# MoE kernel: the last tile's rows turned first, puts ahead of weight sums, a bank wait moved into the loop, final sums on VectorE alone

## The reference, cut to what matters

```python
    yx = jnp.concatenate([o_hg_x, o_pool_x], axis=-1) @ w_out[l]
    x = x + gt1 * rms_norm(yx, g_post_mix[l])
    hx2 = (rms_norm(x, g_pre_ffn[l]) * (1.0 + sc2) + sh2).reshape(B * S, D)
    # moe(hx2): logits = xt @ w_router + b_router; top 4 of 32, softmax over the four
    # for each token and chosen expert e, with weight w:
    gate = xblk @ w_gate[e] + b_gate[e]
    up = xblk @ w_up[e] + b_up[e]
    gate = jnp.minimum(gate, SWIGLU_LIMIT)
    up = jnp.clip(up, -SWIGLU_LIMIT, SWIGLU_LIMIT)
    h = (up + 1.0) * gate * jax.nn.sigmoid(SWIGLU_ALPHA * gate)
    y = h @ w_down[e] + b_down[e]          # times w, summed over the token's four experts
    x = x + gt2 * rms_norm(y, g_post_ffn[l])
```

## Time and profile before

| | |
|---|---|
| median of 3 runs | 2398.84 us (2397.83 to 2398.97) |
| profiled execution | 2394.5 us, its span 2392.6 us |
| PE busy | 2221.9 us, 93% of the span |
| VectorE, ScalarE, GpSimd busy | 44%, 28%, 16% |
| matmuls of `gate_up` (L1753) | 9216, 1007.7 us busy |
| matmuls of `down` (L1786) | 9216, 508.7 us busy |
| chain that ended last, share of PE | 85% |

### The profile page before, as it was taken

The page is one execution under the profiler, slowest core; times in us unless marked ns, Lnnn a source line. Parts: engine busy times, 40 slices in busy tenths (PEclk is TensorE's granted clock), DMA queues, the critical chain, the costliest instruction groups (busy, mean ns, idle before and its releaser), DMA issues.

```text
span 2392.6 us, 57077 instructions
## 1 busy us (share of the span) xinstructions
PE 2221.9 (93%) x21767; PEld 1176.8 (49%) x21768; DVE 1043.4 (44%) x1664; ACT 668.5 (28%) x1414; POOL 376.6 (16%) x491
## 2 busy tenths in 40 slices
PE   5999999998996599999999999999998999999982
PEld 3485765867454244545445454444443444444441
DVE  4154547445346344434434443443353444433334
ACT  5111222233344332222322222322232222222222
POOL 5000000000014212111111121111122112211111
PEclk9999999999997699999999999999999999999996
DMA  9112011126205294967979788888887897888864
GB/s 302 35 36 72 26 33 48 31 67 246 93 36 202 90 373 127 360 211 279 338 250 344 251 313 314 287 305 287 286 328 272 303 340 271 309 291 337 322 216 157
DMA packets 187702, 525.54 MB, mean 220 GB/s; under 512 B 20330, under 2 KB 68066, under 8 KB 187490
## 3 DMA queue, kind: packets, MB, share of 16 engines
q1 hardware_dynamic: 133874, 338.86, 37.7%
q10 hardware_dynamic: 36240, 134.29, 14.4%
q0 software_dynamic: 17536, 51.69, 9.6%
HBM read 486.21 MB, written 38.57 MB: 219 GB/s over the span
## 4 chain that ended last, share of the span: by engine, by line
PE 85%; DMA 6%; DVE 4%; issue 1%; ACT 1%; POOL 1%; ACTq 0%; SPq 0%; POOLq 0%; DVEq 0%
PE ps L1753 40%; PE ps L1786 19%; PE ps L1536 6%; PE ps L1637 5%; PE ps L1532 5%; DMA w_gu_e<-in_w_up_dram 4%; PE ps L1542 2%; PE ps L1593 2%; PE ps L1539 2%; PE ps L1615 1%; PE ps L1656 1%; PE ps L1508 1%; DMA w_down_e<-in_w_down_dram 1%; DVE box L1107 0%; DVE y_all L1460 0%
## 5 line engine op out<-in xcount | busy, mean ns | idle before, releaser
L1753 PE MATMUL ps<-w_gu_e,xT 128*32 128x512 f32 x9216 | 1007.7, 595 | 34.3 <-DVEq L1418 16.6
L1753 PEld LDWEIGHTS ps<-w_gu_e,xT 128*32 128x32 f32 x9216 | 355.9, 110 | 667.4 <-issue 667.1
L1786 PE MATMUL ps<-w_down_e,hT 128*32 128x256 f32 x9216 | 508.7, 380 | 13.4 <-ACT yrow L932 8.4
L1786 PEld LDWEIGHTS ps<-w_down_e,hT 128*32 128x32 f32 x9216 | 351.3, 110 | 181.8 <-issue 40.8
L1383 DVE STREAM_TRANSPOSE gu_t<-ps 128x1024 f32<-128x1024 f32 x94 | 111.9, 1229 | 639.4 <-PE ps L1753 639.4
L914 ACT ACTIVATE xT<-xr,fm 128x128 f32<-128x128 f32 x392 | 184.1, 490 | 569.0 <-PE ps L1753 544.6
L1369 DVE TENSOR_SCALAR yrow<-ps,slot_tab 32x256 f32<-32x256 f32 x376 | 181.3, 482 | 259.0 <-PE ps L1786 167.9
L932 ACT ACTIVATE yrow<-ps,slot_tab 32x256 f32<-32x256 f32 x384 | 179.4, 467 | 352.2 <-issue 235.9
L655 POOL DMA_INDIRECT xg<-xn_rows,idx_g x196 | 197.4, 1007 | 85.4 <-issue 47.6
L649 POOL TENSOR_TENSOR idx_g<-slot_tab,base_row 128x4 int32<-128x4 int32 x49 | 9.2, 189 | 1101.6 <-DVE xr L1405 1087.5
L1536 PE MATMUL ps<-hxT,w_ring 128*128 128x512 f32 (+1 forms) x384 | 142.5, 529 | 3.7 <-ACT hxT L802 3.7
(11 more groups left out here) (301 smaller groups left out, 1515.2 us busy)
## 6 DMA issues: line engine op xcount, KB each, us to landing
w_gu_e<-in_w_gate_dram SPq DMA_DIRECT2D x256, 512.0 KB, 10.7
w_gu_e<-in_w_up_dram SPq DMA_DIRECT2D x256, 512.0 KB, 11.6
w_down_e<-in_w_down_dram ACTq DMA_DIRECT2D x124, 1024.0 KB, 9.2
w_ring<-in_w_ada_dram SPq DMA_DIRECT2D x17, 1024.0 KB, 5.2
w_ring<-in_w_in_dram SPq DMA_DIRECT2D x20, 512.0 KB, 5.2
w_first<-in_w_ada_dram SPq DMA_DIRECT2D x7, 1024.0 KB, 12.2
x_all<-in_x_dram SPq DMA_DIRECT2D x2, 2048.0 KB, 10.6
w_out<-in_w_out_dram SPq DMA_DIRECT2D x8, 512.0 KB, 8.6
```

What stands on the lines that cost most here:

```text
L1753: last = T.matmul(ps[j * GROUP:(j + 1) * GROUP, g, :].rearrange("p (w b f) -> p w b f", w=2, f=GROUP), xT[:, k, g * GROUP:(g + 1) * GROUP] ...
L1786: last = T.matmul(ps[j * GROUP:(j + 1) * GROUP, 4 + g // 2, g % 2 * QUARTER:(g % 2 + 1) * QUARTER], hT[:, g, k, :], w_dn[:, k, j * QUARTER ...
```

## The change

It does five things.

1. For the last tile, PE turns the rows of tile 7 first, then does places(5) and logits(6). VectorE does place(5) ahead of choose(6), and ScalarE exponents(5) ahead of the copy of tile 7, without calling the square root in between.
2. GpSimd puts the slots of tiles 5, 6 and 7 in a row, and sums their weights behind them.
3. PE no longer waits for all 16 copies of the first rows ahead of the loop. ScalarE raises `gu_evac` by 2 when it has issued the last of them, and the waits on `gu_evac` in `gate_up` and on VectorE are 2 higher.
4. `down` asks for size > 0 first, around the rest, and `apart` stands behind all branches, where it stood only in that of size 0 and 1.
5. The final sums are all VectorE's: y * gain for each tile as it lands, into a buffer of its own, `yg_all`; then, by group, yg * rstd + x in one instruction. The groups are of 2, 3 and 3 tiles instead of 1, 2, 2 and 3.

```diff
@@ -157,7 +157,7 @@
         r = region(0, 64)
         w_gu = r("w_gu_e", 2, KT, D)
         w_dn = region(72, 104)("w_down_e", KT, D)
-        y_all = region(0, 32)("y_all", TL, D)
+        y_all, yg_all = region(0, 32)("y_all", TL, D), region(32, 64)("yg_all", TL, D)
 
         r = region(141, 149)
         xg, xr = r("xg", GROUPS, QUARTER), r("xr", GROUPS, KT, GROUP)
@@ -352,8 +352,7 @@
         Y0_BANK = (4, 5, 2, 3)
         TAB_AT, ORD_AT = 0, 4 * NTAB
 
-        FIN = ((0, 1), (1, 3), (3, 5), (5, 8))
-        FIN_POOL = (2, 4, 6)
+        FIN = ((0, 2), (2, 5), (5, 8))
 
 
         vec_in, x_in, misc_in = sem("vec_in"), [sem(f"x_in{k}") for k in range(3)], sem("misc_in")
@@ -395,8 +394,8 @@
             sem(n) for n in ("w_full_ready", "wT_psum", "wT_ready", "y0_psum", "y0_ready"))
         b_dn_in, y0_out = sem("b_dn_in"), [sem(f"y0_out{b}") for b in range(len(y0_sb))]
         y_added = sem("y_added")
-        fin_sq, fin_scaled, fin_dve, fin_pool, out_done = (
-            sem(n) for n in ("fin_sq", "fin_scaled", "fin_dve", "fin_pool", "out_done"))
+        fin_sq, fin_gained, fin_dve, out_done = (
+            sem(n) for n in ("fin_sq", "fin_gained", "fin_dve", "out_done"))
 
 
         Y_ZERO = 1
@@ -531,10 +530,7 @@
             for t in range(TL):
                 sp.dma_start(y_all[:, t, :], y_dram[t * P:(t + 1) * P, :]).then_inc(y_in[t], 16)
             for t in range(TL):
-                if t in FIN_POOL:
-                    sp.wait_ge(fin_pool, FIN_POOL.index(t) + 1)
-                else:
-                    sp.wait_ge(fin_dve, sum(u not in FIN_POOL for u in range(t + 1)))
+                sp.wait_ge(fin_dve, t + 1)
                 sp.dma_start(out[0, t * P:(t + 1) * P, :], x1[:, t, :]).then_inc(out_done, 16)
             sp.wait_ge(out_done, 16 * TL)
 
@@ -631,8 +627,12 @@
                 G.tensor_tensor(w_full[:, t, :], w_j[:, 0, :], w_j[:, 1, :], ALU.add).then_inc(w_full_ready, 1)
                 pool.wait_ge(w_full_ready, t + 1)
 
-            for t in range(TL):
+            for t in range(TL - 3):
                 put_slots(t)
+                spread_weights(t)
+            for t in range(TL - 3, TL):
+                put_slots(t)
+            for t in range(TL - 3, TL):
                 spread_weights(t)
             for k in range(2):
                 pool.wait_ge(xn2_out[k], 16 * TL // 2)
@@ -683,9 +683,6 @@
             scatter(n_before)
             scatter(n_last)
             pool.wait_ge(xg_in, n_last * (16 * GROUPS) + 3 * 16 * GROUPS)
-            for t in FIN_POOL:
-                pool.wait_ge(fin_scaled, t + 1)
-                G.tensor_tensor(x1[:, t, :], x1[:, t, :], y_all[:, t, :], ALU.add).then_inc(fin_pool, 1)
 
 
         @block.scalar
@@ -872,9 +869,11 @@
                 root(ROOT_YX + 1 + 2 * t, 0, 1)
                 if t >= 3:
                     exponents(t - 3)
+                if 3 <= t < TL - 1:
                     A.activation(rs_s[:, 39:40], ones[:, 0:1], ACT.Sqrt)
+            exponents(TL - 3)
             transposed_tile(TL - 1)
-            for t in range(TL - 3, TL):
+            for t in range(TL - 2, TL):
                 exponents(t)
 
             def weights_turned(t0, nt):
@@ -903,6 +902,7 @@
             first_rows(0)
             weights_turned(4, 4)
             first_rows(4)
+            act.sem_inc(gu_evac, 2)
 
             def rows_scaled(m):
 
@@ -1268,8 +1268,8 @@
                     choose(t - 2)
                 if t >= 3:
                     place(t - 3)
+            place(TL - 3)
             choose(TL - 2)
-            place(TL - 3)
             choose(TL - 1)
             place(TL - 2)
             place(TL - 1)
@@ -1382,7 +1382,7 @@
                 for half in range(2):
                     V.transpose(guT[:, 2 * half:2 * half + 2].rearrange("p g w b i -> p (g w b i)"),
                                 ps[:, 2 * half:2 * half + 2, :].rearrange("p a n -> p (a n)")).then_inc(gu_evac, 1)
-                dve.wait_ge(gu_evac, m * 2 + 2)
+                dve.wait_ge(gu_evac, m * 2 + 4)
                 both = guT[:].rearrange("p g w b i -> p g (w b) i")
                 g, u = (guT[:, :, w].rearrange("p g b i -> p g (b i)") for w in range(2))
                 lk(V.tensor_tensor(both, both, biasT[:, :, bass.ds(e, 1)].unsqueeze(1).to_broadcast(
@@ -1445,10 +1445,19 @@
                 ins.then_inc(dve_chain, 1)
                 dve.wait_ge(dve_chain, done + (base + n_tail[0]))
 
+            def gained(lo, hi):
+
+                for t in range(lo, min(hi, TL)):
+                    dve.wait_ge(y_in[t], 16)
+                    V.tensor_tensor(yg_all[:, t, :], y_all[:, t, :], gain[1][:], ALU.mult).then_inc(fin_gained, 1)
+
+            gained(0, FIN[0][1])
             for g, (lo, hi) in enumerate(FIN):
+                gained(lo + 1 if g else hi, hi)
                 dve.wait_ge(fin_sq, hi)
                 c_ = slice(lo, hi)
                 V.tensor_scalar(rs_v[:, c_], ssq[:, c_], 1.0 / D, EPS, ALU.mult, ALU.add).then_inc(var_ready, 1)
+                gained(hi, hi + 1)
                 dve.wait_ge(root_ready, ROOT_YX + 2 * TL + g + 1)
                 lk(V.reciprocal(rs_s[:, c_], rs_s[:, c_]))
                 lk(V.tensor_tensor(rs_t[:, c_], rs_s[:, c_], rs_s[:, c_], ALU.mult))
@@ -1456,12 +1465,9 @@
                 lk(V.tensor_scalar(rs_t[:, c_], rs_t[:, c_], -0.5, 1.5, ALU.mult, ALU.add))
                 lk(V.tensor_tensor(rstd[:, c_], rs_s[:, c_], rs_t[:, c_], ALU.mult))
                 for t in range(lo, hi):
-                    y = y_all[:, t, :]
-                    V.scalar_tensor_tensor(out=y, in0=y, scalar=rstd[:, t:t + 1], in1=gain[1][:], op0=ALU.mult,
-                                           op1=ALU.mult).then_inc(fin_scaled, 1)
-                    if t not in FIN_POOL:
-                        dve.wait_ge(fin_scaled, t + 1)
-                        V.tensor_tensor(x1[:, t, :], x1[:, t, :], y, ALU.add).then_inc(fin_dve, 1)
+                    dve.wait_ge(fin_gained, t + 1)
+                    V.scalar_tensor_tensor(out=x1[:, t, :], in0=yg_all[:, t, :], scalar=rstd[:, t:t + 1],
+                                           in1=x1[:, t, :], op0=ALU.mult, op1=ALU.add).then_inc(fin_dve, 1)
 
 
         @block.tensor
@@ -1704,14 +1710,14 @@
                     if t >= 2:
                         pe.wait_ge(yx_used, t - 1)
                     yx(t, K_EARLY + K_LATE).then_inc(yx_psum, 1)
-                if 1 <= t < TL:
+                if 1 <= t <= TL:
                     turned_rows(t - 1)
+                if t == TL:
+                    places(t - 3)
                 if 2 <= t < TL + 2:
                     logits(t - 2)
-                if t >= 3:
+                if t >= 3 and t != TL:
                     places(t - 3)
-                if t == TL:
-                    turned_rows(t - 1)
             pe.wait_ge(cum_ready, TL)
             T.matmul(ps[:, 0, TL * NE:(TL + 1) * NE], ones_bf[:], cum_bf[:, TL - 1, :], start=True, stop=True
                      ).then_inc(pos_psum, 1)
@@ -1727,7 +1733,7 @@
 
             def gate_up(m, loaded, size):
 
-                pe.wait_ge(gu_evac, m * 2)
+                pe.wait_ge(gu_evac, m * 2 + 2)
                 apart(pe)
                 with pe.If(size > 1):
                     with pe.If(size > 2):
@@ -1764,17 +1770,17 @@
                 pe.wait_ge(yr_ready, n)
                 pe.wait_ge(yv_ready, n)
                 apart(pe)
-                with pe.If(size > 1):
-                    with pe.If(size > 2):
-                        with pe.If(size == 4):
-                            down_of(loaded, (2, 3), False)
-                        with pe.Else():
-                            down_of(loaded, (2,), False)
-                    down_of(loaded, (0, 1), True)
-                with pe.Else():
-                    with pe.If(size > 0):
+                with pe.If(size > 0):
+                    with pe.If(size > 1):
+                        with pe.If(size > 2):
+                            with pe.If(size == 4):
+                                down_of(loaded, (2, 3), False)
+                            with pe.Else():
+                                down_of(loaded, (2,), False)
+                        down_of(loaded, (0, 1), True)
+                    with pe.Else():
                         down_of(loaded, (0,), True)
-                    apart(pe)
+                apart(pe)
 
             def down_of(loaded, groups, ends):
 
@@ -1792,7 +1798,6 @@
 
             pe.wait_ge(tables, 1)
             n_rounds = rounds(pe)
-            pe.wait_ge(y0_ready, 2 * TL)
             with pe.Fori(0, n_rounds) as n:
                 pair = item_pair(pe, n)
                 down(n, (pair >> 12) * 16, (pair >> 3) & 7)
```

## The result

| | before | after |
|---|---|---|
| median | 2397.93 us (2395.40 to 2398.97, 8 runs) | 2404.57 us (2402.02 to 2407.37, 8 runs) |
| profiled execution, span | 2392.6 us | 2401.5 us |
| last `down` matmul ends | 2345.9 | 2360.3 |
| first loop matmul starts | 807.2 | 804.1 |

The changed kernel takes 1.0029 times as long as the one before (95% interval 1.0018 to 1.0039): it is 6.6 us slower, where 6.6 us less was forecast. All ratios in this document leave out two executions in a slower state, one of 6080 us in e6 and one of 2475.7 us of the kernel before, measured with e9 to e12.

A forecast was written before the change was run, and what follows sets the result against it. The prediction took PE's two matmul lines in the expert loop as the bound, so only edges and joints could move: -7.8 (start) + 6.5 (joints) - 5.3 (final sums) = -6.6, from 2398.8 to 2392.2 us, range 2384 to 2398.

The forecast's parts named there:

- Router, 2.3: Router's last tile: turning tile 7's rows first lets its logits start 2.3 us earlier.
- Bank wait out of line, 3.3: Ahead of the loop: PE loads and branches without waiting for the bank copies, 3.3 us earlier.
- Slot table, 2.2, not in the sum: GpSimd's puts ahead of the sums: slot table 2.2 us earlier, bounds 0.9 and 3.7, not setting the loop's start.
- One branch instead of two, 2.2: Ahead of the loop: empty item 0 of `down` branches once, not twice, saving 2.2 us.
- the front: Up to the first loop matmul: router 2.3, bank wait 3.3 and branch 2.2 make it 7.8 us earlier.
- Start of the loop: Prediction's part on the first loop matmul: the sequencer's branches, not data, set it; it moves from 807.22 to 799.4.
- Joints, 5.4 + 1.1: Between `down` and `gate_up` in the loop: added steps cost 5.4 us, added compares 1.1, together +6.5.
- Final sums, -5.3: End of the kernel: with the sums all on VectorE, the last x is written 5.3 us earlier.
- Rival A: Loop joints: the added step costs nothing, issued while `down`'s last matmuls are in the array; 2385.7 us, chance 0.22.
- rival C: Loop joints: each added step costs 0.41 us; 2408 with all compares, 2400.7 in a milder form; chance 0.08, half each.
- B: Start of the loop: the single jump costs as much as two, start gains 4.5 not 7.8; 2395.5 us, chance 0.20.

The follow-up runs named there:

- e6: The kernel before with only the bank wait moved out of PE's queue into `gate_up`: 2396.22 us, 0.9991.
- e9: The changed kernel with the code of `down` for size 1 written ahead of that for larger sizes: 2395.69 us, 0.9988 of before.
- e12: The changed kernel with 64 added semaphore steps in PE's queue ahead of the tables' diagonals: 2403.01 us, 1.0030 of before.
- e1: The changed kernel with the old `down` (two nested branches, `apart` only behind size 0 and 1): 2387.31 us, 0.9959 of before.
- e3: The kernel before with `apart` behind all branches of `down`, without the outer branch: 2400.91 us, 1.0016.
- e4: The kernel before with the new final sums alone: 2390.95 us, 0.9976.
- e5: The kernel before with only the router's new order and the puts ahead of the sums: 2396.59 us, 0.9994.
- e10: e1 without the semaphore step between the wait for gu_evac and the branches of `gate_up`: 2384.53 us, 0.9945 of before.
- e11: e10 also without the semaphore step ahead of the first eight matmuls of `gate_up` (k = 0): 2378.95 us, 0.9919 of before.
- e2: The kernel before with the new `down` alone (outer branch and `apart` behind all branches): 2412.13 us, 1.0066.
- e7: The changed kernel with the outer branch of `down` kept, but `apart` only behind size 1: 2399.86 us, 1.0010 of before.
- e8: The changed kernel with 128 added semaphore steps in PE's queue behind the first rows: 2417.06 us, 1.0084 of before.

## Why the prediction was wrong

The profile of the instruction transfers (queue, packets, MB, share) of the kernel before, and then of the changed one:

```profile
q8 instruction: 33, 0.54, 0.1%
```

```profile
q8 instruction: 38, 0.62, 0.1%
```

Five more pieces of code are brought: 0.08 MB, 16 KB each. The same row for stretches: 790 to 845, where the loop begins, before and after, then 845 to the end, after:

```profile
q8 instruction: 6, 0.10, 0.9%
```

```profile
q8 instruction: 5, 0.08, 0.7%
```

```profile
q8 instruction: 6, 0.10, 0.0%
```

Before, six pieces serve the whole loop, and none comes behind 815. After, five come at first, and six more from 848 to 879, in the third and fourth round. The count parts all the kernels by their jump: the seven that keep the two branches (e1, e3, e4, e5, e6, e10 and e11) have 33, those with the outer branch have 38 (e2, e7, e9) or, with the added steps ahead of the loop, 40 (e8, e12).

- **Router, 2.3: right** as a chain (2.35 in the traces); alone it is worth 1.3.
- **Bank wait out of line, 3.3: right together with the router, too large alone.** The two gave 5.5 for 5.6 in e1. Alone the wait is worth 1.7, and the branch that then comes earlier takes longer (5.78 for 3.60).
- **Slot table, 2.2, not in the sum: too large.** The first xr is written 51.6 us behind tile 7's rows, for 52.2 before. It cost nothing, as the data still weren't what set the start.
- **One branch instead of two, 2.2: right as far as it went.** It saves 3.1 alone (e2) and 2.1 in the changed kernel. With the others the front gave 8.1 for 7.8.
- **The step that failed** is in "Start of the loop": "I take 2.2, nearest to the row that spans a like distance." The two long branches were read, rightly, as code that isn't there yet. But what they fetched was counted as waste to be saved. In the kernel before the second of them, at the branch in front of size 1, is part of what brings the loop's code in during the first round. Leaping over it puts the price off to the third round, and adds to it. There, by the traces, the standstills are 5.7 and 3.2 longer than at the same joints before, and the clock that falls behind them costs 3.1 on 64 matmuls and 2.95 on 128: **15.0 us**, of which the prediction has nothing. e7 against e1 measures it: 12 us, with the 2 to 3 that the single branch saves at the start (2.9 by these two traces) taken off.
- **Joints, 5.4 + 1.1: right in the gaps, somewhat large in what is left of them.** The gaps grew by 6.5 at the joints from `down` and by 0.75 at the others. In e3 they grew by 6.0, waits for weights took back 2.2 (8.9 for 11.1), and +3.8 to +4.6 was left. In the changed kernel such waits took back 4.1. Rival A (hidden) falls, and so does rival C (0.41 per step): 6.0 over 40 steps is 0.15.
- **Final sums, -5.3: right**, -5.4 in e4 and -5.5 in the traces.
- **The rivals** had the slower side at the wrong place: C, with a chance of 0.04 in the form that is slower, put it on the step, at over twice its price, where it was in the branch that the sum had booked as a gain. B falls with the front's 8.1. With 15.0 added, the sum of the prediction would have been +8.4; measured +6.6.

The Trainium skill (Runtime: NRT & Kernel Launch, Instruction fetch mechanics) has the rule that was weighed in the prediction: a taken branch to code that isn't resident forces a fetch. The runs agree with it (6.1 us in e2, 0.21 in e3 at the same branch). The same rule, followed one round further, would have pointed to a loss there: what the jump leaps over may not be brought either. How large it is, only the runs tell.

**What stays open.** Six pieces serve the whole loop before, and the changed kernel brings eleven for the same code, so about five of them must be pieces that had been there or that are brought without need. Which pieces are given up at the leap, and why two shorter jumps keep them, no run here shows. That it is the leap's length, and not something else about the outer branch, is a reading of these runs: none has the outer branch with a short leap.

## What to carry to other kernels

A long branch on first use is not always a cost to be removed; it may be one to be placed: it should fall where the engine waits anyway, and a path that leaps over the rest of a loop's body only moves it to where the engine is busy and its clock has to come back. Before removing such a branch, ask which later round relies on what it brought. And where an engine's sequencer arrives just in time, each step added at a joint or taken away shows in the gap in full, 0.15 us here, but the next wait (here, for weights) takes part of it back in both directions: 2.2 of 6.0 in e3, 3.1 of 6.7 in e10.

## What the runs showed of the hardware

- A branch to code that isn't there took 3.0 to 4.8 us wherever the DMA share during it was 0.36 or less, over all the profiles. With the gathers and the first rows under way, at a share of 0.7 to 0.9 ahead of the loop, it took 4.4 (e7) to 6.2 (e9), and at 1.03 in the loop, beside the weights, 5.9 (e9) to 7.0 (e8). Two branches of 1.7 to 1.8 at 1.03 (e8, e9) had their piece on its way already. The same branch, once its code had come, took 0.07 to 0.28.
- Standstills of PE cost more behind them. Two of 5.5 and 3.4 us in the changed kernel made the matmuls behind them 6.1 us longer (6.77 for 3.66, 16.89 for 13.94), at a mean granted clock of 0.67 over the ten microseconds behind the first; single ones of 5.7 (e9) and 7.1 (e8) made the 128 behind them 2.6 and 2.1 longer.
- VectorE's small step over 128x2 next to a GpSimd add over 128x1024 took 1.92 us, and 0.16 in every group once GpSimd had no part in the end.
